# Two-layer HGRN2 / GLA decoder step: another layout for the GLA sample rows, their state products and the moves of their states

## The reference, cut to what matters

```python
S_t = diag(exp(log_f_t)) S_{t-1} + k_t v_t^T      # state, kept in HBM between steps
o_t = S_t^T q_t                                   # token t included
# evaluated over the 4 tokens at once:
o     = att @ v + (q * exp(b)) @ S                # att: causal scores with decay
S_new = exp(b_last) * S + (k * exp(b_last - b))^T v
```

## Time and profile before

| | |
|---|---|
| runs | 3076.22 us median of 3 (3073.29 to 3076.69) |
| profiled execution | 3078.22 us, span 3076.4 us |
| TensorE busy | 3014.1 us, 98% of the span |
| VectorE, ScalarE, GpSimd busy | 1734.4, 1305.1 and 299.0 us |
| mean granted TensorE clock | 0.992 |
| DMA | 685.60 MB, mean 223 GB/s |

### The profile page before, as it was taken

One profiled execution on the slowest core, in us unless ns is written; L12 is line 12 of the kernel. 1 busy time (PEld: TensorE's weight loads), 2 busy tenths in 40 slices (PEclk: granted clock), 3 DMA queues, 4 the chain that ended last, 5 costly groups with the idle time before them and its releaser, 6 DMA issues. The chain is left out here.

```text
span 3076.4 us, 65619 instructions
## 1 busy us (share of the span) xinstructions
PE 3014.1 (98%) x26670; PEld 2831.1 (92%) x26670; DVE 1734.4 (56%) x2478; ACT 1305.1 (42%) x1712; POOL 299.0 (10%) x291
## 2 busy tenths in 40 slices
PE   7899999999999999999999999999999999999999
PEld 3689999989899999999999899998999999999998
DVE  2577766765744444444445767766664454454545
ACT  1455555553533343333333544544354343343433
POOL 0112111111300000000001402210130000000001
PEclk8899999999999999999999999999999999999999
DMA  9888888888786686776875875675575555555552
GB/s 376 278 267 261 257 269 272 273 291 267 261 284 209 212 261 213 236 239 205 259 247 172 271 236 183 195 239 181 172 245 165 165 167 167 165 166 165 165 165 93
DMA packets 541653, 685.60 MB, mean 223 GB/s; under 512 B 22236, under 2 KB 469268, under 8 KB 541084
## 3 DMA queue, kind: packets, MB, share of 16 engines
q1 hardware_dynamic: 485650, 627.66, 63.5%
q10 hardware_dynamic: 55732, 54.01, 5.4%
HBM read 650.91 MB, written 30.67 MB: 222 GB/s over the span
## 5 line engine op out<-in xcount | busy, mean ns | idle before, releaser
L1998 DVE TENSOR_TENSOR w_lo<-raw,w_hi 128x1024 fp32r<-128x1024 f32 x804 | 991.4, 1236 | 1147.0 <-ACT w_hi L1366 1143.8
L1366 ACT ACTIVATE w_hi<-raw 128x1024 fp32r<-128x1024 f32 x804 | 849.7, 1059 | 1490.3 <-PE main L615 1183.5
L613 PE MATMUL main<-a_hi,w_hi 128*128 128x288 f32 x4224 | 1273.6, 302 | 8.1 <-DVE a_lo L2554 7.2
L615 PE MATMUL main<-a_hi,w_lo 128*128 128x288 f32 x4224 | 1248.6, 296 | 0.0
L614 PE MATMUL main<-a_lo,w_hi 128*128 128x288 f32 x4224 | 1248.3, 296 | 0.0
L613 PEld LDWEIGHTS main<-a_hi,w_hi 128*128 128x128 f32 x4224 | 795.7, 188 | 43.2 <-issue 26.8
L614 PEld LDWEIGHTS main<-a_lo,w_hi 128*128 128x128 f32 x4224 | 796.1, 188 | 4.5 <-issue 1.9
L615 PEld LDWEIGHTS main<-a_hi,w_lo 128*128 128x128 f32 x4224 | 796.0, 188 | 0.0
L615 PE MATMUL main<-act_hi,w_lo 128*128 128x288 f32 x2048 | 604.9, 295 | 0.0
L614 PE MATMUL main<-act_lo,w_hi 128*128 128x288 f32 x2048 | 604.6, 295 | 0.0
L613 PE MATMUL main<-act_hi,w_hi 128*128 128x288 f32 x2048 | 603.6, 295 | 0.0
(11 more groups left out here) (351 smaller groups left out, 2013.9 us busy)
## 6 DMA issues: line engine op xcount, KB each, us to landing
raw<-in_w_ada SPq DMA_DIRECT2D x384, 512.0 KB, 4.9
raw<-in_w_up SPq DMA_DIRECT2D x256, 512.0 KB, 4.6
raw<-in_w_down SPq DMA_DIRECT2D x256, 512.0 KB, 3.6
raw<-in_hg_w_in SPq DMA_DIRECT2D x128, 512.0 KB, 6.6
raw<-in_gla_w_in SPq DMA_DIRECT2D x100, 512.0 KB, 4.4
raw<-in_hg_w_out SPq DMA_DIRECT2D x32, 512.0 KB, 8.1
gl_s<-in_state_gla ACTq DMA_DIRECT2D x32, 512.0 KB, 5.4
out_new_gla_sample<-gl_s ACTq DMA_DIRECT2D x32, 512.0 KB, 4.4
```

Source lines behind the costliest of these rows:

```text
L613: mm(out, hi, x_hi[:, kb, :], start=kb == 0, stop=False)
L615: last = mm(out, lo, x_hi[:, kb, :], start=False, stop=kb == KB - 1)
L1366: F(w_hi[:, st.split_slot(g)].rearrange("p k n -> p (k n)"), raw[:, slot, :], ACT.Copy).then_inc(hi_ready, 1)
L1998: V.tensor_tensor(w_lo[:, s].rearrange("p k n -> p (k n)"), raw[:, slot, :], w_hi[:, s].rearrange("p k n -> p (k n)").bitcast(F32), ALU.su ...
```

## The change

The sample rows of GLA are laid 32 to two sequences: each of four groups of 32 rows holds the 8 tokens of two neighbouring sequences four times, as terms (zero or value, high part, low part), for keys (`gl_sk`) and values (`gl_sv`). The terms are now made by DVE before the turn (`gl_value_rows` in step 17, and the end of `gl_key_mul` in step 19); the turn gives 128 rows. `gl_vx`, a copy of the turned values in the space of `pre`, serves the sample outputs, so `gl_gates` moves from step 6 to 7 and waits for them. Two masks (`pmask`, even and odd sequences) take the place of eight.

A call of `gl_sample(n, k)` now makes half j of the states of two sequences: two products over 32 rows each, in two row groups and into two banks. `gl_state` does the same two; loads and stores move half a state (256 KB) in a DMA. Read-outs 0 and 1 stand in step 23, read-outs 2 and 3 in step 5. Scores of levels 0 to 2 are made in four column groups for 8 tokens each, and copied in four pieces.

```diff
+    gl_vx = gl["pre"][:, :, :].rearrange("p j t -> p (j t)")[:, 0:GLA_V]
-    gl_sk = mem.put("gl_sk", [P, 2, 3, TS], at=mem.start["gl_kt"])
-    gl_sv = mem.put("gl_sv", [P, 4, 3, TS], at=mem.start["gl_ksm"])
+    gl_sk = mem.put("gl_sk", [P, 2, P], at=mem.start["gl_kt"])
+    gl_sv = mem.put("gl_sv", [P, 4, P], at=mem.start["gl_ksm"])
...
+    def term_rows(rows, c):
+        return rows.rearrange("p a (g c i) -> p a g c i", g=4, c=4)[:, :, :, c, :]
...
             if L <= 2:
                 for j in range(2):
-                    sample_scores(32 * L, lhs[:, j, TP:T], rhs[:, j, TP:T], j == 0, j == 1)
+                    for g in range(4):
+                        own = slice(TP + 8 * g, TP + 8 * g + 8)
+                        mm(b6[32 * g:32 * g + 8, 32 * L + 8 * g:32 * L + 8 * g + 8], lhs[:, j, own], rhs[:, j, own],
+                           start=j == 0, stop=j == 1, skip_group_check=True, tile_position=(0, 32 * g))
...
-            for b in (2 * q, 2 * q + 1):
-                pe.wait_ge(G["s0_loaded"][b % 4], 32 * n + 16 * (b // 4 + 1))
+            if q % 2 == 0:
+                for loaded in G["s0_loaded"]:
+                    pe.wait_ge(loaded, 64 * n + 32 * (q // 2 + 1))
...
-        def gl_sample(n, b):
-            pe.wait_ge(G["s_masked"], 8 * n + b + 1)
-            if b == 0:
+        def gl_sample(n, k):
+            pair, j = divmod(k, 2)
+            if k == 0:
+                pe.wait_ge(G["s_masked"], 2 * n + 2)
...
-            for j, bank in enumerate((b4, b5)):
-                last = mm(bank[:, :], gl["ksm"][:, b % 2, j, :], gl["vs"][:, :], start=True, stop=True)
+            for i, bank in enumerate((b4, b5)):
+                g = 2 * (pair // 2) + i
+                r = slice(32 * g, 32 * g + 32)
+                last = mm(bank[:, :], gl["ksm"][r, pair % 2, j, :], gl["vs"][r, :], start=True, stop=True,
+                          tile_position=(32 * g, 0))
...
-                if s in (1, 4, 5):
-                    gl_read_out(pn, 1 if s == 1 else s - 2)
+                if s == 5:
+                    gl_read_out(pn, 2)
+                    gl_read_out(pn, 3)
...
                     gl_read_out(n, 0)
+                    gl_read_out(n, 1)
                     gl_sample(n, 0)
...
+        def pair_sequences(pair):
+            return [4 * (pair // 2) + pair % 2 + 2 * i for i in range(2)]
+        def gl_load(n, pair, j):
+            for b in pair_sequences(pair):
+                act.dma_start(gl["s0"][:, b % 4, j], gl_state[cols(n, 1), b, :, j, :].rearrange("h k v -> (h k) v")
+                              ).then_inc(G["s0_loaded"][2 * (pair % 2) + j], 16)
+        def gl_store(n, k):
+            pair, j = divmod(k, 2)
+            act.wait_ge(G["ss_read"], 8 * n + k + 1)
+            for i, b in enumerate(pair_sequences(pair)):
+                act.dma_start(gl_state_out[cols(n, 1), b, :, j, :].rearrange("h k v -> (h k) v"), gl["s1"][:, i, j]
+                              ).then_inc(G["s_stored"][j], 16)
...
-                        gl_load(pn, s + 4)
-                if own and 5 <= s <= 8:
-                    gl_load(n, s - 5)
+                        gl_load(pn, 2 + s // 2, s % 2)
+                if own and 6 <= s <= 9:
+                    gl_load(n, (s - 6) // 2, s % 2)
...
-            step(V.tensor_tensor(gl_sk[:, :], threefold(gl["x"][:, 1, :, TP:T]), threefold(gl["k"][:, :, TP:T]), ALU.mult))
...
+            src = token_groups(gl["x"][:, 1, :, TP:T])
+            V.memset(term_rows(gl_sk, 0), 0.0)
+            V.tensor_copy(term_rows(gl_sk, 2).bitcast(F32R), src)
+            step(V.tensor_copy(term_rows(gl_sk, 1).bitcast(F32R), src))
+            V.tensor_tensor(term_rows(gl_sk, 3).bitcast(F32R), src, term_rows(gl_sk, 1), ALU.subtract).then_inc(G["s_split"], 1)
...
             if L <= 2:
-                for q in (0, 32):
-                    V.copy_predicated(gl["atts"][q:q + 32, :], masks[q:q + 32, L, :],
-                                      b6[q:q + 32, 32 * L:32 * L + 32])
+                for g in range(4):
+                    r, own = slice(32 * g, 32 * g + 8), slice(8 * g, 8 * g + 8)
+                    V.copy_predicated(gl["atts"][r, own], masks[r, L, 0:8],
+                                      b6[r, 32 * L + 8 * g:32 * L + 8 * g + 8])
...
-                if s <= 5:
-                    gl_mask(pn, s + 2)
...
-                    sample_split(G, 2 * n + 1, [(gl["vs"][32:64, :], b6[32:64, :])])
+                    dve.wait_ge(G["s_turned_read"], 2 * n + 1)
+                    V.tensor_copy(gl_vx, b6[:, :]).then_inc(G["s_split"], 1)
```

More of the change, by code:

```diff
@@ L262, in build_program @@
     bmask = mem.put("bmask", [P, NB])
+    pmask = mem.put("pmask", [P, 2])
     b_ada_at = mem.at
@@ L489, in mixer_stores @@
         elif i == 2:
-            mixer_stored(engine, G, GLA_HEADS * NB // 2, GLA_HEADS * 2)
+            mixer_stored(engine, G, GLA_HEADS * NB, GLA_HEADS * 2)
     block = nc.Block()
@@ L1135, in gl_turn_vs @@
             pe.wait_ge(G["turned_read"], 3 * n + 1)
+            pe.wait_ge(G["s_split"], 3 * n + 1)
             for j in range(4):
-                last = turn_samples(b6, j * P, gl_sv[:, j])
+                last = turn(b6[:, j * P:(j + 1) * P], gl_sv[:, j], ident[:, :])
             last.then_inc(G["s_turned"], 1)
@@ L1149, in gl_turn_k @@
             pe.wait_ge(G["turned_read"], 3 * n + 2)
+            pe.wait_ge(G["s_split"], 3 * n + 2)
             for j in range(2):
-                last = turn_samples(b7, j * P, gl_sk[:, j])
+                last = turn(b7[:, j * P:(j + 1) * P], gl_sk[:, j], ident[:, :])
             last.then_inc(G["s_turned"], 1)
@@ L1892, in gl_step @@
                     panel_done(GLA, n, s - 1)
-                    F(gl_sv[:, 2 * j:2 * j + 2], threefold(panel(GLA, 2 + j)[:, :, TP:T]), ACT.Copy)
                     F(gl["v"][:, 2 * j:2 * j + 2, :], panel(GLA, 2 + j), ACT.Copy).then_inc(panel_read["A"], 1)
@@ L2117, in _ @@
         V.tensor_copy(masks[:, :, :], boot["masks"][:, :, :]).then_inc(masks_set, 1)
+        step(V.tensor_tensor(pmask[:, :], bmask[:, 0:2], bmask[:, 2:4], ALU.add))
+        step(V.tensor_tensor(pmask[:, :], pmask[:, :], bmask[:, 4:6], ALU.add))
+        step(V.tensor_tensor(pmask[:, :], pmask[:, :], bmask[:, 6:8], ALU.add))
         dve.wait_ge(a_ready, 4)
@@ L2211, in gl_key_mul, with gl_value_rows @@
             last.then_inc(G["kd_ready"], 1)
+            src = token_groups(gl["x"][:, 1, :, TP:T])
[3 more added lines that the diff above has]
+            V.tensor_tensor(term_rows(gl_sk, 3).bitcast(F32R), src, term_rows(gl_sk, 1), ALU.subtract).then_inc(G["s_split"], 1)
+        def gl_value_rows(n):
+            dve.wait_ge(panel_read["A"], GLA.emptied(n, 3)[1])
+            src = token_groups(gl["v"][:, :, TP:T])
+            V.tensor_copy(term_rows(gl_sv, 0), src)
+            V.tensor_copy(term_rows(gl_sv, 3).bitcast(F32R), src)
+            step(V.tensor_copy(term_rows(gl_sv, 1).bitcast(F32R), src))
+            V.tensor_tensor(term_rows(gl_sv, 2).bitcast(F32R), src, term_rows(gl_sv, 1), ALU.subtract).then_inc(G["s_split"], 1)
         def hg_gate(n):
@@ L2681, in gl_spread, with gl_mask, gl_state @@
             last.then_inc(G["att_spread"], 1)
-        def gl_mask(n, b):
-            if b >= 2:
-                dve.wait_ge(G["ss_done"], 8 * n + b - 1)
-            V.tensor_scalar(gl["ksm"][:, b % 2], gl["ks"][:, :, :].bitcast(F32), bmask[0:96, b:b + 1], None, ALU.mult
+        def gl_mask(n, parity):
+            V.tensor_scalar(gl["ksm"][:, parity], gl["ks"][:, :, :].bitcast(F32), pmask[:, parity:parity + 1], None, ALU.mult
                             ).then_inc(G["s_masked"], 1)
-        def gl_state(n, b):
-            dve.wait_ge(G["ss_done"], 8 * n + b + 1)
-            if b >= 2:
-                dve.wait_ge(G["s_stored"][b % 2], 64 * n + 16 * (b // 2))
-            for j, bank in enumerate((b4, b5)):
-                last = V.scalar_tensor_tensor(out=gl["s1"][:, b % 2, j, :], in0=gl["s0"][:, b % 4, j, :],
+        def gl_state(n, k):
+            pair, j = divmod(k, 2)
+            dve.wait_ge(G["ss_done"], 8 * n + k + 1)
+            dve.wait_ge(G["s0_loaded"][2 * (pair % 2) + j], 64 * n + 32 * (pair // 2 + 1))
+            if pair:
+                dve.wait_ge(G["s_stored"][j], 128 * n + 32 * pair)
+            for i, bank in enumerate((b4, b5)):
+                b = 4 * (pair // 2) + pair % 2 + 2 * i
+                last = V.scalar_tensor_tensor(out=gl["s1"][:, i, j, :], in0=gl["s0"][:, b % 4, j, :],
                                               scalar=gl["dec"][:, j, b:b + 1], in1=bank[:, :],
@@ L2746, in gl_step @@
                     gl_read(n, s - 11, prev)
+                if s == 17:
+                    gl_value_rows(n)
                 if s == 19:
```

47 lines of the change are left out of this document (20 added, 27 removed).

## The result

| kernel | median, us | ratio to before, 95% interval | profiled run: time / span, us |
|---|---|---|---|
| before | 3075.6 (3073.3 to 3077.4, 6 runs) | | 3078.2 / 3076.4 |
| after | 3088.4 (3084.9 to 3090.1, 6 runs) | 1.0042 [1.0031, 1.0052] | 3089.2 / 3087.4 |

The change makes the kernel slower by 12.8 us. The forecast was +4.0 (3080.2, range 3071.5 to 3087.5), a change too small to see; the result lies above the range.

A forecast was written before the change was run, and what follows sets the result against it. TensorE, busy for 98% of the span, was taken to bound the kernel. The terms 3.0 - 3.3 + 1.1 + 1.75 + 1.8 - 0.3 = +4.0 us led from a median of 3076.2 to 3080.2, range 3071.5 to 3087.5.

The forecast's parts named there:

- A: GLA heads: six of eight state-product pairs a head stand alone, row-tiled at 0.60 us instead of 0.46; +3.0 us.
- B: GLA read-outs joined two by two: 2.45 us with a pair instead of 2.86, twice a head; -3.3 us.
- C: Sample scores, levels 0 to 2: eight more small product rows of 11.5 ns in 12 levels; +1.1 us.
- D: Levels 0 to 2: four DVE copies instead of two make PE wait, mainly before level 5; +1.75 us (0 to 4).
- E: Step 4, three heads: PE asks sooner for the fifth state, which hangs on a store; +1.8 us (0 to 3.5).
- F: Last head's tail: masks leave DVE, -0.3 us, with -2 to +3 for the clock.
- (1): Row-tile switch is free, waits of D and E taken up elsewhere: 3067.6 us, or 3070.8 with them; chance 0.09.
- (2): State-product pairs: fp32r row groups don't overlap or weights load in turn; +6.8 us, 3087; chance 0.11.
- bound of -0.21 for a free switch: Lower bound of A for each lone pair if switching to row tiles cost nothing; -5.0 us in all.
- wait of 0.45 before level 5: Part of D: PE's new wait for DVE's level 5 factors, about 0.45 us in each of three heads.
- rival (3): Half-state moves land later; PE waits at three heads' fifth state and twice in the tail; +3.8 us, 3084; chance 0.18.
- The sign that I had named for it: Stores holding DVE longer than 14.6 us in all would show rival (3).

The follow-up runs named there:

- e10: e2 with each row-tiled pair of state products issued twice; 3089.05 us, ratio 1.0046 to before.
- e4: Before with read-outs 0 and 1 joined in step 23, 2 and 3 in step 5, next head's loads one step later; 3079.0 us, ratio 1.0016.
- e6: Before with each masked copy of the sample scores at levels 0 to 2 split by columns into two; ratio 1.0003.
- e9: Before with each masked copy of the sample scores at levels 0 to 2 split by columns into three; 3076.9 us, ratio 1.0009.
- e15: Before with each load and store of a sample state made as two transfers of 256 KB, old order kept; 3077.5 us, ratio 1.0011.
- e8: e2 with stores of sample states cut to the first 64 of 512 columns; 3075.7 us, ratio 1.0004 to before.
- e11: Before with stores of sample states cut to the first 64 of 512 columns; 3072.05 us, ratio 0.9993.
- e1: Before with 32 unused bytes a partition set aside behind bmask, where pmask would stand; 3080.0 us, ratio 1.0019.
- e2: After with pmask put into 8 unused bytes behind eps, so that no buffer moves; 3082.6 us, ratio 1.0027 to before.
- e14: Before with 32 unused bytes directly in front of act_hi, moving act_hi, act_lo and the scratch buffers behind; 3080.7 us, ratio 1.0022.
- e3: After with each load and store as one 512 KB DMA for two sequences' halves; 3085.3 us, ratio 1.0034 to before.
- e7: Before with the key mask for state b+2 issued ahead of state b+1 on DVE; 3072.8 us, ratio 0.9996.
- e5: Before with an unused buffer of 64 bytes a partition behind bmask; 3074.35 us, ratio 1.0002.
- e13: Before with 32 unused bytes a partition behind act_lo, moving most scratch buffers but not act_hi and act_lo; ratio 1.0003.

## Why the prediction failed, step by step

| step | forecast, us | profiles of before and after | what the runs say |
|---|---|---|---|
| A, pairs alone | +3.0 | 24 x 0.164 = +3.9 | switch 0.39 and stream 0.23 (e10) |
| B, joined read-outs | -3.3 | 8 x 0.36 = -2.9 | 2.51 for two and a pair (e4) |
| C, sample scores | +1.1 | 0 | level 3: 1.02 before, 1.01 after |
| D, copies | +1.75 | +2.3 | doses (e6, e9) |
| E, states in steps 3 to 5 | +1.8 | +2.7 in three heads | halves and lost cover (e15, e4) |
| F, tail, beyond A and B | -0.3 | about +1 | stores (e8, e11) |
| `act_hi`, `act_lo` moved | none | +3.4 | +3.9 to +6.6 (e1, e2, e14) |

A is a difference such as 2.34 - 2.18 in the table of steps; B is 2.48 + 0.62 for steps 23 and 1, less the 0.16 of A, against 1.65 + 1.65. The column of the profiles sums to 10.4 of the 11.0 us.

**The step that failed first is one that is not there.** The text says that `pmask` "is made once in an idle stretch" and takes it as time on DVE. Its 8 bytes take 32 in memory, every buffer put after it moves, and stages without any change pay for it. By medians it is 3.9 us of the 12.8, 6.2 where the shift stands alone; with it alone the forecast of +4.0 would have been at +7.9, still 4.9 short of the result.

**A and B were right in mechanism and near in size.** The entry and exit price read from L1317 was 0.37, it is 0.39, and the rivals (1) and (2) of the prediction fall. The Trainium skill, "TensorEngine Tiling (Array Packing)", section "Tiling Modes", has a change of mode drain the engine and gives no price; the trace agrees with a price of 0.39 us. For B the saving was 0.36, not 0.41. Together they cost 1.0 us where the sum had a gain of 0.3. (The recorded bound of -0.21 for a free switch is a slip: 0.13 less 0.37 is -0.24. It would move rival (1) by 0.8 us, and nothing else.) C was a term too many: the eight added products of 8 columns cost nothing, and the 11.5 ns of a row of 32 columns was the wrong row to price them from.

**D was right in mechanism and a third too small.** A copy of 8x8 takes 0.172 from start to start (0.69 for four) where I had 0.165, and the 0.27 us (0.18 in the first head) by which C was to delay TensorE, and so to soften the pauses, do not exist. The wait of 0.45 before level 5 was also not what its own figures give: 1869.97 + 0.84 less 1870.17 + 0.27 is 0.37. Measured were 0.56, 0.54 and 0.48.

**E named the wrong state.** I put the wait at the fifth state, in step 4. After has its pauses in step 3: 1.08, 0.83 and 0.58 us in three heads (1.70, 1.45 and 1.20, less 0.62), and in step 5, 0.04, 0.46 and 0.21 for a load of the read-outs. Less the 0.52 of before that is +2.7. The halves bring the step 3 pause: e15 has it in the old order (0.61 and 1.58). That is rival (3), to which I gave 0.18 and which I kept out of the likeliest sum: its condition, a store 0.45 us later, was met (7.8 us and 8.9 against 6.6, above). The sign that I had named for it did not show: DVE waited 12.9 us for stores in after and 12.2 in e15, not over 14.6. It was a poor sign, since seven profiles with the old order and whole moves have 9.2 to 16.6; what counts is the one wait at the fourth state. The lost cover is the other part (e4: +5.2 with whole moves and the old pairs). The parts can't be split by medians: 1.3 us from after to e3, 3.3 from before to e15, intervals of some 3 us each. Nor do they add: 3.3 and 5.2, the latter after a gain of B's size, are more than the 5.2 that hang on whole stores. The wait for a read-out's load was named only as something that "none of my steps has".

**F was too good.** I took -0.3 us for masks that leave DVE (e7 confirms at most a small gain) and left the clock as a margin. The tail of after, PE:

```profile
2117.95 0.50 PE L1209 MATMUL bank<-gl_vs,gl_ksm 32*128 32x512 f32 x2 [2.08 <-DVE gl_s L2740]
...
2123.67 0.50 PE L1209 MATMUL bank<-gl_vs,gl_ksm 32*128 32x512 f32 x2 [1.22 <-DVE gl_s L2740]
2128.39 0.50 PE L1209 MATMUL bank<-gl_vs,gl_ksm 32*128 32x512 f32 x2 [2.43 <-DVE gl_s L2740]
2131.75 3.64 PE L1191 MATMUL bank<-gl_s,gl_suf 128*32 128x512 f32 x16 [0.75 <-DMA gl_s<-in_state_gla]
2135.32 0.79 PE L1209 MATMUL bank<-gl_vs,gl_ksm 32*128 32x512 f32 x2
```

and its windows (as the earlier trace rows):

```profile
2129.00:2132.00 3.00, 2.25 (x16) 1.88 (x20) 1.88 (x3) 0.00 (x0) 0.00 (x0) 0.70 1.06 387
2132.00:2135.00 3.00, 3.00 (x16) 0.46 (x8) 0.00 (x0) 0.00 (x0) 0.00 (x0) 0.50 0.91 311
2135.00:2138.00 3.00, 3.00 (x17) 2.25 (x14) 1.84 (x3) 0.60 (x1) 0.00 (x0) 0.67 0.09 30
```

6.5 us of pauses instead of 4.1, and behind the last ones TensorE is granted 0.50 of its clock, 1.2 GHz: the joined read-outs that follow take 3.64 us instead of 1.92. So the gain of a join was paid back once, right behind the pause. But the clock does not tell after from before: from 2100 to 2150 us its mean is 0.93 in both profiles, and 0.97 or 1.00 in the other six with the old order. The profile of before was a poor yardstick here: from the last head's step 23 to the end of that head it took 46.1 us, and the six other kernels with the old order and whole stores (e1, e5, e6, e9, e13, e14) took 43.3 to 45.0; after took 47.4, e2 45.1, e3 47.2. Against those six the tail of after is 2.4 to 4.1 us longer, not 1.3, which would make F the largest miss beside the shift. This stretch can account for medians that differ by 12.8 us where profiles differ by 11.0.

**What is left open.** Of the 6 us that a shift of 32 bytes costs, 3.4 are in the spacing of the products, and the rest has no place yet. How the loss at the stores divides into halves and order, in the heads and above all in the tail, is not settled either: halves have e15 and the profile of e3, the order has e4. A third slot for finished states, which would take the waits for stores away without cutting them, was not tried; a slot takes 4096 bytes a partition.

## What to carry over

Count what a new buffer does to the addresses of those behind it: here that was 3.9 to 6.2 us of 12.8, in stages that nobody had edited. Where a stage is paced by stores and loads, time saved on the engine ahead of them can come back as a wait behind them, so a read-out that stands in front of a waiting product is cover, and moving it is not free. And moves split into two made the next user of the buffer wait longer, +3.3 us with the old order, although the bytes were the same. Last, a single profile is a weak yardstick for a stretch that varies: compare several of kernels that share it.

## What the runs showed of the hardware

- Streamed fp32r operands moved by 32 bytes made three products of 288 columns take 400.0 ns instead of 398.3 (e1, e14, after); moved by 64 they took 397.8 (e5). The kernel was 6 us longer with the shift of 32 and no longer with that of 64.
- Entering and leaving row tiles costs 0.39 us for two products of 512 columns, which then run side by side in 0.23 (e10).
- A masked copy took 0.19 us for 32x32, 0.125 for 32x16 and 0.107 for 32x11, but 0.172 for 8x8 in four quadrants in turn; whether shape or quadrant makes the last was not separated.
- Products of 8 columns in four column groups added nothing where four of 32 columns were turned into eight (the stretch of levels 2 and 3: 1.02 us before, 1.01 after).
- With two transfers of 256 KB in place of one of 512 KB, a state's store held its buffer for 6.7 to 8.9 us (e15, after; fourth state of three heads) where it was free within 6.6 before, and after 5.7 to 7.4 in e3 (whole moves, new order).
